# Last output projection of a two-layer streaming encoder step: five tile pairs by seven block products, weight sums by accumulating DMAs, one masked copy per level

## The reference

```python
for layer in range(DEPTH):                       # DEPTH = 2, D_MODEL = 2048
    hp = rms_norm(xp, norm_w[layer])             # 512 prompt frames; hs: 32 sample frames
    qa, ka, va, g = jnp.split(hp @ w_in[layer], 4, axis=-1)
    op = mixer(...) * jax.nn.silu(g)             # attention or HGRN2, 16 heads of 128
    xp = xp + op @ w_out[layer]                  # the output projection
    xs = xs + osm @ w_out[layer]
```

## Time and profile before

| | us |
|---|---|
| median of 3 runs | 2374.85 (2374.75 to 2374.86) |
| profiled execution | 2374.45 |
| its span, first to last instruction | 2372.7 |
| mean granted TensorE clock, share of full speed | 0.996 |
| TensorE busy | 2333.4 |
| VectorE busy | 1252.3 |
| ScalarE busy | 1021.1 |
| Pool busy | 96.2 |

### The profile page before, as it was taken

One profiled execution on the slowest core, in us unless ns is written; L12 is line 12 of the kernel. 1 busy time (PEld: TensorE's weight loads), 2 busy tenths in 40 slices (PEclk: granted clock), 3 DMA queues, 4 the chain that ended last, 5 costly groups with the idle time before them and its releaser, 6 DMA issues. The chain is left out here.

```text
span 2372.7 us, 46285 instructions
## 1 busy us (share of the span) xinstructions
PE 2333.4 (98%) x18457; PEld 2310.9 (97%) x18457; DVE 1252.3 (53%) x2278; ACT 1021.1 (43%) x1386; POOL 96.2 (4%) x95
## 2 busy tenths in 40 slices
PE   7999999999999999999999999999999999998999
PEld 6999999999999999899999999999999999997999
DVE  6444444444444444432357777777777777776221
ACT  5444444444444444532344444444444444444221
POOL 6000000000000000310100000000000000003000
PEclk9999999999999999999999999999999999998999
DMA  7333222222222222254532222222222222212542
GB/s 236 100 87 87 85 85 85 85 85 85 85 85 85 85 85 83 62 156 116 143 91 75 74 73 69 71 73 74 69 71 73 74 74 74 74 48 57 149 118 78
DMA packets 388088, 211.29 MB, mean 89 GB/s; under 512 B 9091, under 2 KB 378294, under 8 KB 388022
## 3 DMA queue, kind: packets, MB, share of 16 engines
q1 hardware_dynamic: 340182, 181.19, 26.8%
q10 hardware_dynamic: 47872, 29.64, 4.1%
HBM read 186.41 MB, written 24.38 MB: 89 GB/s over the span
## 5 line engine op out<-in xcount | busy, mean ns | idle before, releaser
L474 PE MATMUL psum<-act_hi,w_hi 128*128 128x272 f32 x5120 | 1081.5, 293 | 13.5 <-DVE act_lo L1152 5.3
L474 PE MATMUL psum<-act_hi,w_lo 128*128 128x272 f32 x5120 | 1063.1, 289 | 0.0
L474 PE MATMUL psum<-act_lo,w_hi 128*128 128x272 f32 x5120 | 1060.0, 289 | 0.0
L1143 DVE TENSOR_TENSOR w_lo<-w_raw,w_hi 128x1024 fp32r<-128x1024 f32 x320 | 400.5, 1252 | 859.3 <-ACT w_hi L785 859.2
L474 PEld LDWEIGHTS psum<-act_hi,w_hi 128*128 128x128 f32 x5120 | 805.7, 189 | 16.6 <-DVE act_lo L1152 4.4
L474 PEld LDWEIGHTS psum<-act_lo,w_hi 128*128 128x128 f32 x5120 | 807.9, 189 | 0.0
L474 PEld LDWEIGHTS psum<-act_hi,w_lo 128*128 128x128 f32 x5120 | 803.4, 190 | 0.0
L785 ACT ACTIVATE w_hi<-w_raw 128x1024 fp32r<-128x1024 f32 x320 | 338.0, 1057 | 680.8 <-PE psum L474 634.7
L785 ACT ACTIVATE work<-work 128x544 f32<-128x544 f32 (+2 forms) x368 | 261.4, 723 | 313.0 <-DVE work L1266 198.7
L785 ACT ACTIVATE work<-psum 128x512 f32<-128x512 f32 (+5 forms) x256 | 111.3, 483 | 148.8 <-PE psum L465 115.1
L450 POOL TENSOR_TENSOR act_lo<-full,act_hi 128x544 fp32r<-128x544 f32 x24 | 37.1, 1548 | 1905.5 <-DVE act_lo L1152 1876.5
(11 more groups left out here) (205 smaller groups left out, 1710.3 us busy)
## 6 DMA issues: line engine op xcount, KB each, us to landing
w_raw<-in_w_in SPq DMA_DIRECT2D x256, 512.0 KB, 4.0
w_raw<-in_w_out SPq DMA_DIRECT2D x64, 512.0 KB, 6.3
out<-work ACTq DMA_DIRECT2D x48, 256.0 KB, 2.4
x_residual<-work ACTq DMA_DIRECT2D x32, 272.0 KB, 3.8
work<-x_residual SPq DMA_DIRECT2D x32, 272.0 KB, 3.0
full<-in_x_prompt SPq DMA_DIRECT2D x3, 1024.0 KB, 11.5
work<-in_cache_k ACTq DMA_DIRECT2D x16, 128.0 KB, 2.3
work<-in_cache_v ACTq DMA_DIRECT2D x16, 128.0 KB, 4.1
```

Source lines behind the costliest of these rows:

```text
L474: mm = pe.matmul(acc[par][:, j, :], w[:, slot, k % KH, :], a[:, k, j * HT:(j + 1) * HT], start=(k == 0 and n == 0), stop=(k == KT - 1 and ...
L1143: dve.tensor_tensor(w_lo[:, slot], w_raw[:, slot], w_hi[:, slot].bitcast(F32), ALU.subtract).then_inc(lo_ready, 1)
```

## The change

The last five of the eight pairs (q = 0 to 4) are made in another way. The 2048 x 256 weight block of a pair is seen as 2 x 2 quarters (two halves of the rows, two tiles of columns), the activation as 2 x 2 blocks (two halves of its rows, two halves of its columns). The four output blocks, eight block products before, are made from seven, each of 8 row tiles x 3 splits = 24 matmuls of 272 columns. Pairs 0 to 2 stay as they are (`PLAIN = 3`).

- Four of the products need differences of activation blocks (T1 to T4). VectorE makes them, ScalarE rounds them, VectorE makes the remainders, all once, during pairs 1 and 2. They lie in places that are free by then (`Y`, `full`, `work`).
- Four of the products need sums of weight quarters. SP loads one quarter into a buffer, and Pool issues DMAs that add another quarter from HBM into it (`accum_op=ALU.add`). For one pair that is a chain of three additions into one buffer (used after the first for product 0, after the second for product 3, after the third for product 6) and a single addition for product 2. Two chain buffers alternate. The signs are in the sums behind the products.
- Weights are split in pieces of half a quarter, 128 x 512, two for each product, numbered through; pieces n of a pair below count from 0 to 13. Seven places are used in rotation, so piece n is split when TensorE has finished piece n - 7. ScalarE makes the high part (`piece_split`), VectorE the remainder (`piece_rest`).
- VectorE makes the two output tiles from four PSUM banks by nine sums of 272 columns (`add_up`, counted by `fast_added`). TensorE waits for some of them before it uses a bank again: product 5 for the second sum, product 6 for the third.
- In the mixer the four masked copies of a level become one of 256 columns, with the mask repeated by a step of zero. The copy for the sample stays.

```diff
+PLAIN = 3
+FAST = KT // 2 - PLAIN
+PRODUCTS = 7
+PIECES = 7
+EVACS = 9
...
+        w_sum = nc.alloc_sbuf_tensor_at("w_sum", [P, KH, P], F32, offset=w_lo_at)
...
+        t1_hi = nc.alloc_sbuf_tensor_at("t1_hi", [P, KH, HT], F32R, offset=Y_at)
...
+        FAST_B = [T1, B11, T3, T2, B21, T4, B22]
+        def fast_banks(q):
+            z, x, w, y = [psum[:, i, 0:HT] for i in ((0, 1, 2, 3), (3, 1, 2, 0))[q % 2]]
+            return z, x, w, y
...
+        QUARTERS = {1: (0, 0, 0), 2: (1, 1, 0), 4: (2, 0, 1), 5: (3, 1, 1)}
...
+        def chain_raw(q):
+            return (w_sum[:], w_raw[:, 0])[q % 2]
...
+            def load_quarter(q, idx):
+                n, row, kh = quarter(q, idx), QUARTERS[idx][1], QUARTERS[idx][2]
+                if n < 3:
+                    sp_eng.wait_ge(lo_ready, OUT1 + 4 * PLAIN - 2 + n)
+                else:
+                    q_, idx_ = (n - 3) // 4, (1, 2, 4, 5)[(n - 3) % 4]
+                    sp_eng.wait_ge(piece_lo_ready, split_of(q_, idx_))
+                sp_eng.dma_start(quarter_raw(n), weights(q, row, kh)).then_inc(quarter_loaded[n % 3], 16)
+            def load_chain(q):
+                if q == 0:
+                    sp_eng.wait_ge(half_done, OUT1 + 4 * PLAIN - 3)
+                elif q == 1:
+                    sp_eng.wait_ge(lo_ready, OUT1 + 4 * PLAIN - 3)
+                else:
+                    sp_eng.wait_ge(piece_lo_ready, split_of(q - 2, 6))
+                sp_eng.dma_start(chain_raw(q), weights(q, 1, 0)).then_inc(chain_loaded[q % 2], 16)
+            load_quarter(0, 1)
+            load_chain(0)
+            load_quarter(0, 2)
+            for q in range(FAST):
+                if q + 1 < FAST:
+                    load_chain(q + 1)
+                load_quarter(q, 4)
+                load_quarter(q, 5)
+                for par in range(2):
+                    n = 2 * (PLAIN + q) + par
+                    if q == 0:
+                        sp_eng.wait_ge(evacuated, added(1, n - 2))
+                    else:
+                        sp_eng.wait_ge(fast_added, EVACS * q)
+                    sp_eng.dma_start(x_old[par], x_residual[n]).then_inc(x_old_loaded[par], 16)
+                if q + 1 < FAST:
+                    load_quarter(q + 1, 1)
+                    load_quarter(q + 1, 2)
...
+            def add_to_chain(q, row, kh):
+                pool.dma_start(chain_raw(q), weights(q, row, kh), accum_op=ALU.add).then_inc(chain_added[q % 2], 16)
+            for q in range(FAST):
+                pool.wait_ge(chain_loaded[q % 2], 16 * (q // 2 + 1))
+                add_to_chain(q, 1, 1)
+                n = quarter(q, 2)
+                pool.wait_ge(quarter_loaded[n % 3], 16 * (n // 3 + 1))
+                pool.dma_start(quarter_raw(n), weights(q, 0, 0), accum_op=ALU.add).then_inc(quarter_added, 16)
+                pool.wait_ge(piece_lo_ready, split_of(q, 0))
+                pool.wait_ge(chain_added[q % 2], 48 * (q // 2) + 16)
+                add_to_chain(q, 0, 0)
+                pool.wait_ge(piece_lo_ready, split_of(q, 3))
+                pool.wait_ge(chain_added[q % 2], 48 * (q // 2) + 32)
+                add_to_chain(q, 0, 1)
...
+            def product(q, idx):
+                b_hi, b_lo = FAST_B[idx]
+                z, x, w_, y = fast_banks(q)
+                bank, fresh = (z, x, w_, y, x, w_, z)[idx], idx < 4
+                for half_ in range(2):
+                    n = 2 * (PRODUCTS * q + idx) + half_
+                    r = n % PIECES
+                    pe.wait_ge(piece_lo_ready, n + 1)
+                    for kk in range(KP):
+                        k = half_ * KP + kk
+                        for m, (w, a) in enumerate(((piece_hi(r), b_hi), (piece_hi(r), b_lo), (piece_lo(r), b_hi))):
+                            if q == 0 and m == 0:
+                                if idx == 0:
+                                    pe.wait_ge(diff_lo_ready, k + 1)
+                                elif idx == 2:
+                                    pe.wait_ge(diff_lo_ready, KH + 2 * k + 2)
+                                elif idx == 3:
+                                    pe.wait_ge(diff_lo_ready, KH + 2 * k + 1)
+                            mm = pe.matmul(bank, w[:, kk, :], a[:, k, :], start=fresh and k == 0 and m == 0,
+                                           stop=k == KH - 1 and m == 2, skip_group_check=True)
+                    mm.then_inc(piece_done, 1)
...
+            def piece_split(n):
+                q, idx, half_ = n // (2 * PRODUCTS), n // 2 % PRODUCTS, n % 2
+                if idx in (0, 3, 6):
+                    act.wait_ge(chain_added[q % 2], 48 * (q // 2) + 16 * (idx // 3 + 1))
+                    raw = chain_raw(q)
+                elif idx == 2:
+                    act.wait_ge(quarter_added, 16 * (q + 1))
+                    raw = quarter_raw(quarter(q, idx))
+                else:
+                    g = quarter(q, idx)
+                    act.wait_ge(quarter_loaded[g % 3], 16 * (g // 3 + 1))
+                    raw = quarter_raw(g)
+                r = n % PIECES
+                if n < PIECES:
+                    act.wait_ge(half_done, OUT1 + 4 * PLAIN - 3 + r // 2)
+                else:
+                    act.wait_ge(piece_done, n - PIECES + 1)
+                func(piece_hi(r), raw[:, half_ * KP:(half_ + 1) * KP, :], ACT.Copy).then_inc(piece_hi_ready, 1)
...
+            for step in range(PRODUCTS * FAST):
+                q, idx = step // PRODUCTS, step % PRODUCTS
+                if 2 * step + 5 < 2 * PRODUCTS * FAST:
+                    piece_split(2 * step + 5)
+                if idx == 2:
+                    act.wait_ge(piece_done, 2 * step)
+                    if q == 0:
+                        act.wait_ge(diff_lo_ready, 3 * KH)
+                    else:
+                        act.wait_ge(fast_added, EVACS * (q - 1) + 1)
+                    func(prod_1, fast_banks(q)[1], ACT.Copy).then_inc(prod_1_copied, 1)
+                if 2 * step + 6 < 2 * PRODUCTS * FAST:
+                    piece_split(2 * step + 6)
+                if idx in (2, 3):
+                    if q == 0:
+                        put_y(PLAIN - 1, idx - 2)
+                    else:
+                        put_fast(q - 1, 3 - idx)
+            put_fast(FAST - 1, 1)
+            put_fast(FAST - 1, 0)
...
-                for b in range(NB):
-                    dst = A[:, b * P:(b + 1) * P].rearrange("p (b j) -> p b j", j=2 * m)[:, :, m:2 * m]
-                    src = M[bank][:, b * 64:(b + 1) * 64].rearrange("p (b j) -> p b j", j=m)
-                    ins = dve.copy_predicated(dst, msk, src)
-                    if b < NB - 1 or m <= SAMPLE // 2:
-                        ch.done(ins)
+                dst = A[:, 0:SEQ].rearrange("p (n b j) -> p n b j", n=NB, j=2 * m)[:, :, :, m:2 * m]
+                src = M[bank][:, 0:NB * 64].rearrange("p (n b j) -> p n b j", n=NB, j=m)
+                ins = dve.copy_predicated(dst, msk.unsqueeze(1).broadcast_to([P, NB, 64 // m, m]), src)
                 if m <= SAMPLE // 2:
...
+            def diffs_234(k):
+                t_3, t_2 = t_sets[k % 2][1:]
+                if k >= 2:
+                    dve.wait_ge(diff_lo_ready, KH + 2 * k - 2)
+                else:
+                    dve.wait_ge(diff_lo_ready, KH)
+                dve.tensor_tensor(t_3, full[:, k, HT:T], full[:, KH + k, HT:T], ALU.subtract).then_inc(diff_made, 1)
+                if k:
+                    diff_2_lo(k - 1)
+                dve.wait_ge(diff_made, KH + 3 * k + 1)
+                dve.tensor_tensor(t_2, t_3, full[:, k, 0:HT], ALU.subtract).then_inc(diff_made, 1)
+                if k:
+                    diff_3_lo(k - 1)
+                dve.wait_ge(diff_made, KH + 3 * k + 2)
+                dve.tensor_tensor(t4_full[:, k, :], full[:, KH + k, 0:HT], t_2, ALU.add).then_inc(diff_made, 1)
...
+            def add_up(step):
+                q, idx = (step - 1) // PRODUCTS, (step - 1) % PRODUCTS
+                base = EVACS * q
+                z, x, w_, y = fast_banks(q)
+                if step == 0 or idx < 3:
+                    return
+                dve.wait_ge(piece_done, 2 * step)
+                def put(n, out, a, b, op=ALU.add):
+                    dve.tensor_tensor(out, a, b, op).then_inc(fast_added, 1)
+                if idx == 3:
+                    dve.wait_ge(prod_1_copied, q + 1)
+                    if q:
+                        dve.wait_ge(fast_added, base)
+                    put(1, part_u, y, prod_1)
+                    dve.wait_ge(fast_added, base + 1)
+                    put(2, part_v, w_, part_u, ALU.subtract)
+                    dve.wait_ge(fast_added, base + 2)
+                    if q == 0:
+                        dve.wait_ge(y_turned, 2 * PLAIN)
+                    else:
+                        dve.wait_ge(y_turned, 2 * (PLAIN + q) - 1)
+                    put(3, x_new[1][:, HT:T], part_v, z, ALU.subtract)
```

(21 more changed lines are left out.)

234 lines of the change are left out of this document (211 added, 23 removed).

## The result

The changed kernel takes 2390.3 us (median of 4 runs, 2388.9 to 2394.7), the kernel before 2374.8: a ratio of 1.0070, 95% interval 1.0058 to 1.0082. It is 15.5 us slower, inside the stated range and on the other side of the forecast. The profiled execution took 2390.84 us, its span 2389.1.

The account below looks back on a forecast made before the run. TensorE was taken to bound the kernel. 2374.45 - 15.0 (products) - 0.5 (masked copies) + 7.55 (stalls on additions) = 2366.5 us profiled, 2366.9 as median; range 2358 to 2394.

Parts of the forecast that it names:

- Products removed: Fast pairs on TensorE: 168 matmuls instead of 192, 22.15 us a pair, five save 15.0 us; one bank costs nothing.
- Masked copies: Mixer's last head: one 256-column copy near 0.44 us, 0.18 less per level, three levels save 0.5 us.
- Differences and plain pairs at nothing: Activation differences during plain pairs 1 and 2: last remainder ready near 30.9 us, wanted at 33.3, so no cost.
- The accumulating DMAs: Pool's additions in fast pairs: 5.9 us alone, 8.5 in traffic, 7.5 taken; stalls at product 5 total 7.55 us.
- L: Time of one accumulating DMA, from Pool's wait being met to its full count; taken as 7.5 us.
- the prediction's own formula: Period of a fast pair's loop, 2L + 9.05 us; 24.05 at 7.5, against TensorE's 22.15.
- The loop: Second and third additions, splits, remainders and sums: holds product 5 about 1.9 us in each of four later fast pairs.
- The engines: Rival: the 16 DMA engines become the bound in fast pairs, 26.0 us a pair, 2376.6 us; chance 0.14.
- The clock: Stalls in fast pairs could lower TensorE's clock; taken as 0, upper end 7 us.
- The sign: Whole kernel: faster 0.52, same 0.19, slower 0.29.
- the point of no change: Loop at product 5 longer than a plain pair: L above 8.05 in steady pairs, about 8.4 with the first's slack.
- the rival with L = 10: Rival: loop at product 5 longer than a plain pair, 29.05 us, 35 lost, 2394 us; long loop's chance 0.22.

Follow-up runs that it names:

- With copies: Changed kernel with Pool's adding transfers made plain copies that overwrite, in the same places and waits: 2370.6 us, ratio 0.9982.
- each reordering: Changed kernel with next pair's first addition ahead of the third: 2393.2 us; store behind piece 13's split: 2387.6; both: 2384.0; store plus two other moves: 2383.4.
- with room on the engines: Changed kernel with store behind piece 13's split, next pair's first addition ahead of the third, three of five plain loads cut to an eighth: 2372.9 us, ratio 0.9998.

## Why the prediction was wrong, point by point

- *Products removed*: right. 24 matmuls take 3.00 us, a fast pair without waits 22.2 against the 22.15 of the sum; the one bank costs nothing.
- *Masked copies*: right in place and kind (0.44 us for a copy), 0.75 instead of 0.5 in the trace.
- *Differences and plain pairs at nothing*: wrong twice. That a remainder now stands ahead of a residual sum was overlooked (2.6 us alone, 3.8 in the changed kernel). And only the last piece of the differences was counted against its date; what they do to the second and third addition of the first fast pair was not. The sum had the second one issued 5.7 us ahead of that pair's start and the third landed at 11.3 us. With copies the third was issued at 9 and landed near 16. In the changed kernel the second was issued 1.8 us ahead, the third at 11.5, and it landed at 20.3: product 5 started 25.5 us after product 0 instead of 16.25.
- *The accumulating DMAs*: the step that failed. An addition was taken as a time of its own, L = 7.5, in one loop to which nothing else belongs, with engines that have room (19.1 us a pair). Alone it takes 7.2 us at 182 GB/s, not the 5.9 of the lower bound; in the loop L was 8.2, and at that L the prediction's own formula gives 25.45 us a pair and about 2374 in all, which is no change.
- *The loop*: right in place, product 5 and the second sum, but one of two. Pool's queue makes another, by the next pair's first addition directly behind the third; it set every second step of the changed kernel and cost some 2.3 us there. And a loop with a fixed L was the wrong model: with full loads each reordering lengthened the landings, and the steps stayed at 26.9 to 27.7 us.
- *The engines*: priced as a rival with 0.14 and treated as apart from L. They are not apart: with room on the engines the same order of instructions needs 23.7 us instead of 27.0. The 26.0 us per pair of that rival are the prediction's nearest number to the 26.9 measured; its 2376.6 is short because it has neither the first plain pair nor the late first fast pair. The DMA share of 1.0 to 1.17 that was named as the engines' mark is there, together with the loop's own mark.
- *The clock*: taken as 0, since TensorE would be early anyway. Of the 6.6 us behind the three stalls this is nearly right for the first two, where the additions were hardly ahead of the slow matmuls. The 1.8 us behind the last stall count in full. No run took the low clock out by itself.
- *The sign*: L in the loop, 8.2, lies within the 8.05 to 8.4 that were named as the point of no change, so it did not decide alone. That the rival with L = 10 gave 2394, near the 2390.3 measured, is in part luck: the additions of the loop were not that long.
- *The gap added up*, from the forecast of 2366.5 to the profiled 2390.84: 7.1 us for L at 8.2 instead of 7.5, 7.9 for the first fast pair beyond that, 4.0 for the four steps behind it (mainly the first additions), 3.8 for the first plain pair and 1.8 for the last low clock, less 0.25 for masked copies worth 0.75 instead of 0.5: 24.4, against the 24.3 measured.

## What to carry to other kernels

Before the time of a transfer that adds stands in a loop, measure its rate alone and see what room it leaves on the DMA engines. When a wait is removed from a loop and little comes back, compare the period of the loop and the time of each transfer in it, before and after: either a second loop of the same length is left, or the transfers have grown by what the wait gave up. Give the engines room in one run to tell the two apart. Here four sums of 1.2 us on an engine with room were cheaper than four adding transfers.

## What the runs showed of the hardware

- An addition of 512 KB from memory into SBUF took 7.2 us in a quiet stretch and 12.5 beside four loads; a copy on the same queue 5.4 to 6.1, and 8.4 beside loads. The queue shows 1040 packets for the addition and 144 for the copy.
- Two additions issued within 1 us of each other, with nothing else on the queue, landed after 6.5 and 11.1 us. In the changed kernel the second one landed after 11.2 to 13.1 us (the first after 6.7 to 9.2), with three of five loads cut to an eighth after 11.0 to 12.9.
- Plain loads that ran beside additions, two of them always under way, took 13.6 us; the same loads without additions 4.2.
- The same sum of 128 x 1024 numbers took VectorE 1.22 us.
